# A chunked state-space scan: the running sums of the decay reach all partitions through memory instead of through TensorE

## The reference, cut to what matters

```python
a_cs = jnp.cumsum(da, axis=-1)
seg = a_cs[..., :, None] - a_cs[..., None, :]
lmat = jnp.exp(jnp.where(causal, seg, -jnp.inf))
y_diag = jnp.einsum("bgrcls,bcsgrp->bclgrp", cb[:, :, None] * lmat, x_dt)
```

## Time and profile before

| | us |
|---|---|
| median of 3 runs | 1354.4 |
| lowest, highest | 1351.99, 1354.83 |
| profiled execution, its own time | 1355.93 |
| its span in the trace | 1354.1 |
| TensorE busy | 1225.2 (90%) |
| VectorE busy | 448.6 (33%) |
| ScalarE busy | 270.8 (20%) |
| GpSimd busy | 195.4 (14%) |

### The profile page before, as it was taken

How to read it: one execution, slowest core, us unless ns; L and a number is a source line. 1 busy time by engine, 2 the same in 40 slices (tenths; PEclk the granted TensorE clock), 3 DMA queues, 4 the chain that set the end, 5 groups by cost and what they waited for, 6 DMA issues and landing times.

```text
span 1354.1 us, 13742 instructions
## 1 busy us (share of the span) xinstructions
PE 1225.2 (90%) x4939; PEld 640.7 (47%) x4939; DVE 448.6 (33%) x985; ACT 270.8 (20%) x656; POOL 195.4 (14%) x316
## 2 busy tenths in 40 slices
PE   3999999888999998999998999999998899978856
PEld 1535865556554445448843444443443344433322
DVE  4576024345556301102773222221212121211116
ACT  2141121122442000000121222221212121211101
POOL 4000011110002000001262122111121212111101
PEclk9999999888999998999998999998998999998978
DMA  9632220112437431218053989999999999999564
GB/s 303 167 125 62 74 82 32 43 52 94 125 113 268 144 129 31 93 62 348 35 202 108 362 315 395 424 422 421 420 419 396 410 405 407 377 417 419 239 254 202
DMA packets 106827, 318.08 MB, mean 235 GB/s; under 512 B 14260, under 2 KB 67592, under 8 KB 80776
## 3 DMA queue, kind: packets, MB, share of 16 engines
q1 hardware_dynamic: 87152, 269.37, 51.6%
q0 software_dynamic: 18080, 43.07, 8.9%
q10 hardware_dynamic: 1528, 4.77, 0.9%
HBM read 310.29 MB, written 26.79 MB: 249 GB/s over the span
## 4 chain that ended last, share of the span: by engine, by line
PE 81%; DVE 6%; DMA 6%; issue 3%; SPq 2%; ACT 1%; POOL 0%; POOLq 0%; ACTq 0%; DVEq 0%
PE ps L1725 21%; PE ps L1573 12%; PE ps L1733 10%; PE ps L1353 7%; PE ps L1361 5%; DMA gu_lo<-in_exp_w_up_dram 4%; PE ps L1601 4%; PE ps L1388 3%; PE ps L1713 3%; PE ps L1546 2%; PE ps L1802 2%; PE ps L1654 2%; PE ps L1510 1%; PE ps L1674 1%; PE ps L1446 1%
## 5 line engine op out<-in xcount | busy, mean ns | idle before, releaser
L1725 PE MATMUL ps<-gu_hi,xsT 128*64 128x512 f32 (+1 forms) x672 | 219.5, 614 | 24.4 <-DMA gu_hi<-in_exp_w_up_dram 11.5
L1725 PEld LDWEIGHTS ps<-gu_hi,xsT 128*64 128x64 f32 (+1 forms) x672 | 85.8, 165 | 136.9 <-issue 136.5
L1272 DVE SCALAR_TENSOR_TENSOR hid<-ps,wgt,gated 128x256 f32<-128x256 f32 x42 | 20.3, 484 | 338.8 <-ACT gated L860 338.8
L1573 PE MATMUL ps<-n1T,ring 128*128 128x512 f32 x256 | 113.0, 603 | 3.7 <-DVE mod L1098 3.0
L1725 PE MATMUL ps<-gu_lo,xsT 128*64 128x512 f32 (+1 forms) x352 | 95.5, 660 | 22.4 <-issue 16.6
L1353 PE MATMUL ps<-n1T,ring 128*128 128x512 f32 x256 | 111.9, 594 | 0.0
L1733 PE MATMUL ps<-dn_hi,hidT 128*64 128x512 f32 (+1 forms) x336 | 108.6, 596 | 0.0
L632 POOL DMA_INDIRECT expert_rows<-hn,meta x42 | 41.7, 994 | 420.7 <-DVE hn L1268 399.7
L860 ACT ACTIVATE gated<-ps 128x256 f32<-128x256 f32 x42 | 16.1, 384 | 331.9 <-PE ps L1725 331.9
L1573 PEld LDWEIGHTS ps<-n1T,ring 128*128 128x128 f32 x256 | 49.4, 194 | 65.6 <-issue 61.7
L1353 PEld LDWEIGHTS ps<-n1T,ring 128*128 128x128 f32 x256 | 48.1, 190 | 58.7 <-issue 58.7
(11 more groups left out here) (325 smaller groups left out, 1383.5 us busy)
## 6 DMA issues: line engine op xcount, KB each, us to landing
gu_hi<-in_exp_w_gate_dram SPq DMA_DIRECT2D x42, 1024.0 KB, 16.7
gu_hi<-in_exp_w_up_dram SPq DMA_DIRECT2D x42, 1024.0 KB, 28.7
dn_hi<-in_exp_w_down_dram SPq DMA_DIRECT2D x42, 1024.0 KB, 23.6
ring<-in_w_in_dram SPq DMA_DIRECT2D x24, 1024.0 KB, 5.6
gu_lo<-in_exp_w_gate_dram SPq DMA_DIRECT2D x22, 1024.0 KB, 14.0
gu_lo<-in_exp_w_up_dram SPq DMA_DIRECT2D x22, 1024.0 KB, 27.1
dn_lo<-in_exp_w_down_dram SPq DMA_DIRECT2D x22, 1024.0 KB, 21.9
h<-in_ada_w_dram POOLq DMA_DIRECT2D x32, 512.0 KB, 4.9
```

The costliest lines, as they stand in the source:

```text
L1573: ins = pe.matmul(ps[:, 4 * jj + b, :], w[:, k, P * jj:P * jj + P], src[:, k, :], start=(k == 0), stop=(k == KC - 1))
L1725: ins = pe.matmul(ps[rows, 2 + b, :], xsT[:, b, k, rows], gu(s)[:, :, k, :], start=(k == 0), stop=(k == KC - 1))
```

## The change

The running sums are also computed by four matmuls after the third z block, one per tile, with `dts` as the stationary side and the triangle as the moving side: 16 rows (one per head) of 128 columns, in bank 7 of PSUM. ScalarE copies them to `summed` (16 partitions, in the room of `attT`). GpSimd stores them to a tensor in memory, `decay_sums`, and loads them back tile by tile with a broadcast over the 128 partitions, 8 KB each, into `decay`, which lies in a part of `raw` that is free after the convolution. The load for tile t + 1 is issued when the subtractions of tile t are done. `sum_rows` is gone, and the subtractions read `decay` in SBUF.

The order in a tile on TensorE becomes: `turn_tile`, `FILL[3t]`, `outputs`, `FILL[3t+1]`, the first four of the eight matmuls of `FILL[3t+2]`, `turn_u`, and the other four. ScalarE's reads of the fills move to fit. The final sums over the experts' rows use the semaphores `x_in` in place of their own `sums_in`, with other counts. The core of the diff:

```diff
+    decay_d = nc.dram_tensor("decay_sums", [T, HEADS, P], F32, kind="Internal").ap()
...
+        decay = flat(raw[:, :, :])[:, PAIRS * SEQ:(PAIRS + T) * SEQ].rearrange("p (h l) -> p h l", h=HEADS)
+        summed = attT[0:HEADS, 0, :]
...
@@ the GpSimd queue, ahead of its loop over tiles and in it @@
+            def spread(t):
+
+                if t >= 1:
+                    pool.wait_ge(seg_done, 2 * t)
+                pool.dma_start(decay.rearrange("p h l -> p (h l)"),
+                               decay_d[t:t + 1].rearrange("t h l -> t (h l)").broadcast_to([P, HEADS * P])).then_inc(decay_in, 16)
+
+            pool.wait_ge(summed_done, 1)
+            pool.dma_start(decay_d.rearrange("t h l -> h t l"), summed.rearrange("h (t l) -> h t l", t=T)).then_inc(summed_out, 16)
+            pool.wait_ge(summed_out, 16)
+            pool.wait_ge(conv_done, NXBC)
+            spread(0)
...
                     pool.tensor_tensor(heads(xdec), heads(xdt), over(ex[:, HEADS:2 * HEADS], HD),
                                        ALU.mult).then_inc(xdec_done, 1)
+                    spread(t + 1)
@@ the ScalarE queue @@
+                    if i == 3 and t == 0:
+                        act.wait_ge(summed_ready, 1)
+                        act.activation(summed, ps[0:HEADS, 7, :], ACT.Copy).then_inc(summed_done, 1)
...
                 act.activation(ex, exarg, ACT.Exp).then_inc(ex_done, 1)
-                for n in FILL[3 * t]:
-                    evacuate(n)
                 for g in range(GROUPS):
...
-                for n in FILL[3 * t + 1]:
+                for n in FILL[3 * t]:
                     evacuate(n)
...
-                for n in FILL[3 * t + 2]:
+                for n in FILL[3 * t + 1] + FILL[3 * t + 2]:
                     evacuate(n)
@@ the VectorE queue @@
+                dve.wait_ge(decay_in, 16 * (t + 1))
+                if t >= 1:
+                    dve.wait_ge(y_ready, t)
                 for g in range(GROUPS):
-                    dve.wait_ge(bc_ready, 2 * t + g + 1)
                     for hh in range(HG):
                         hd = HG * g + hh
-                        ins = dve.tensor_scalar(seg[:, hd, :], ps[:, (6, 2)[g] + hh // 4, P * (hh % 4):P * (hh % 4) + P],
+                        ins = dve.tensor_scalar(seg[:, hd, :], decay[:, hd, :],
                                                 exarg[:, hd:hd + 1], 0.0, ALU.subtract, ALU.min)
                     ins.then_inc(seg_done, 1)
@@ the TensorE queue @@
+                if i == 2:
+                    pe.wait_ge(dtok_done, 1)
+                    for t in range(T):
+                        ins = pe.matmul(ps[0:HEADS, 7, P * t:P * t + P], dts[:, t, 1, :], tri[:, :], start=True, stop=True)
+                    ins.then_inc(summed_ready, 1)
...
-            def sum_rows(t):
-
-                for g in range(GROUPS):
-                    if g == 1:
-                        pe.wait_ge(xtok_done, t + 1)
-                    for hh in range(HG):
-                        ins = pe.matmul(ps[:, (6, 2)[g] + hh // 4, P * (hh % 4):P * (hh % 4) + P],
-                                        dts[:, t, 1, HG * g + hh:HG * g + hh + 1].broadcast_to([P, P]), tri[:, :],
-                                        start=True, stop=True)
-                    ins.then_inc(bc_ready, 1)
...
                 for n in FILL[3 * t]:
                     fill(n)
-                sum_rows(t)
+                outputs(t)
                 for n in FILL[3 * t + 1]:
                     fill(n)
-                outputs(t)
-                for n in FILL[3 * t + 2]:
+                *front, last = FILL[3 * t + 2]
+                for n in front:
                     fill(n)
+                fill(last, range(KC // 2))
                 turn_u(t)
+                fill(last, range(KC // 2, KC))
```

More of the change, by code:

```diff
@@ L318, in hybrid_ssd_swa_moe_adaln_block @@
         xdt_done, xdec_done, skip_done = sem("xdt_done"), sem("xdec_done"), sem("skip_done")
-        bc_ready, seg_done, decay_done, m_done = sem("bc_ready"), sem("seg_done"), sem("decay_done"), sem("m_done")
+        summed_ready, summed_done, summed_out = sem("summed_ready"), sem("summed_done"), sem("summed_out")
+        decay_in, seg_done, decay_done, m_done = sem("decay_in"), sem("seg_done"), sem("decay_done"), sem("m_done")
         y_ready, y_read, state_done = sem("y_ready"), sem("y_read"), sem("state_done")
@@ L350, in hybrid_ssd_swa_moe_adaln_block @@
         ht_ready, hT_done, ey_ready, ey_act, ey_dve = sem("ht_ready"), sem("hidT_done"), sem("ey_ready"), sem("ey_act"), sem("ey_dve")
-        sums_in = [sem(f"sums_in{t}") for t in range(T)]
         tail_sum, fsq_in, fin_done, stored = sem("tail_sum"), sem("fsq_in"), sem("fin_done"), sem("stored")
@@ L473, in _ @@
             for t in range(T):
-                sp.dma_start(gu(t)[:, :, :, :].rearrange("p a k f -> p (a k f)"), rows_v[:, t, 0:4 * D]).then_inc(sums_in[t], 16)
-                sp.dma_start(flat(dn(t)[:, :, :]), rows_v[:, t, 4 * D:]).then_inc(sums_in[t], 16)
+                sp.dma_start(gu(t)[:, :, :, :].rearrange("p a k f -> p (a k f)"), rows_v[:, t, 0:4 * D]).then_inc(x_in[t], 16)
+                sp.dma_start(flat(dn(t)[:, :, :]), rows_v[:, t, 4 * D:]).then_inc(x_in[t], 16)
             for t in range(T):
@@ L1320, in _ @@
                 total = dn(t)[:, 0, :]
-                dve.wait_ge(sums_in[t], 32)
+                dve.wait_ge(x_in[t], (64 if t == 0 else 48))
                 chain(dve.tensor_tensor(total, total, dn(t)[:, 1, :], ALU.add))
@@ L1347, in bank_read, with features, tokens @@
                 return proj_read[n % 2], (n - JOB_Z - (n - JOB_Z) % 2) // 2 + 1
-            def features(n, w, lo):
+            def features(n, w, lo, ks=range(KC)):
                 bank = bank_for(n)
-                for k in range(KC):
+                for k in ks:
                     ins = pe.matmul(bank, w[:, k, lo:lo + P], n1T[:, k, :], start=(k == 0), stop=(k == KC - 1))
-                ins.then_inc(proj_ready, 1)
-                return ins
-            def tokens(n, w, t):
+                if k == KC - 1:
+                    ins.then_inc(proj_ready, 1)
+            def tokens(n, w, t, ks=range(KC)):
                 bank = bank_for(n)
-                for k in range(KC):
+                for k in ks:
                     ins = pe.matmul(bank[:, 0:WB], n1T[:, k, P * t:P * t + P], w[:, k, :],
                                     start=(k == 0), stop=(k == KC - 1))
-                ins.then_inc(proj_ready, 1)
+                if k == KC - 1:
+                    ins.then_inc(proj_ready, 1)
             pe.wait_ge(const, 3)
@@ L1409, in _, with fill @@
                     ins.then_inc(dtok_ready, 1)
-            def fill(n):
+            def fill(n, ks=range(KC)):
                 if n < JOB_K:
                     m = n - JOB_Q
-                    features(n, block_in(BLK_Q + m // 2), P * (m % 2))
+                    features(n, block_in(BLK_Q + m // 2), P * (m % 2), ks)
                 elif n < JOB_V:
-                    features(n, block_in(BLK_K), P * (n - JOB_K))
+                    features(n, block_in(BLK_K), P * (n - JOB_K), ks)
                 else:
-                    tokens(n, block_in(BLK_V), n - JOB_V)
+                    tokens(n, block_in(BLK_V), n - JOB_V, ks)
             def turn_tile(t):
@@ L1797, in _ @@
             for t in range(T):
-                pe.wait_ge(sums_in[t], 32)
+                pe.wait_ge(x_in[t], (64 if t == 0 else 48))
                 rows = gu(t)[:, :, :, :].rearrange("p a k f -> p (a k f)")
```

## The result

| | us |
|---|---|
| before, median of 4 runs | 1353.45 (1351.99 to 1354.83) |
| changed, median of 4 runs | 1334.09 (1332.28 to 1335.10) |
| ratio, with its 95% interval | 0.9844 [0.9827, 0.9860] |
| changed: profiled execution, its span | 1332.7 |

The change takes 19.4 us off the median, and 21.4 us off the span of the profiled executions. The forecast was 1339.8 in a range of 1322 to 1347.

A forecast was written before the change was run, and what follows sets the result against it. TensorE, 81% of the last-ending chain, bounds the kernel; 29.7 - 1.4 - 8.7 - 5 = 14.6 us gain takes the profiled 1355.9 to 1341.3, median put at 1339.8, range 1322 to 1347.

The forecast's parts named there:

- TensorE's own work: In the scan: 14.3 us of broadcasts removed, 0.9 us for four matmuls added, net gain 13.4 us.
- waits ahead of the turned rows: TensorE's idle time before the turned rows of u in tiles 1 to 3 shrinks, gaining 6.4 us.
- waits for the next turned tile, attention's first: Half fill behind the turned rows covers 1.3 us three times, 3.9 us; wait before the attention shrinks by 0.4 us.
- clock behind the old waits: In the scan, slow TensorE work behind the removed idle times returns to faster clock, gaining 5.6 us.
- new waits ahead of the outputs: TensorE waits for the subtractions and products: 1.4 us undisturbed plus 8.7 us from GpSimd delaying VectorE, in tiles 1 to 3.
- clock behind the new waits: Slow clock after the waits before the outputs costs 2 us in tiles 1 and 2, 1 in tile 3: 5 us.
- rival 2: VectorE's subtractions are not held by GpSimd: 28.3 us gain, 1326.1 us, or 1329 at slower subtractions; chance 0.29.
- rival 1: GpSimd's delays of VectorE are real, but the new waits leave the clock up: 19.6 us gain, 1334.8 us; chance 0.16.
- the undisturbed wait: TensorE's wait before the outputs without GpSimd's delays: 0.25 us in tiles 1 and 2, 0.9 in tile 3, together 1.4.
- the attention's slow start: Clock of 0.54 at the attention's start, 331 us, expected to stay because tile 3 keeps a wait of 3.3 us.
- Rival 3: The broadcast load from memory is far slower than a block, making the kernel slower: 1363.8 us at 30 us each; chance 0.04.
- The one-to-one count past the scan: Time saved in the scan reaches the kernel's end in full, since later stages and their transfers move with it.

The follow-up runs named there:

- experiment 1: The changed kernel with GpSimd's two products of a tile held back until the tile's 16 subtractions are done; 1328.93 us, ratio 0.9807.
- experiment 9: The changed kernel with only GpSimd's skip product held back until the subtractions are done; 1335.31 us, ratio 0.9840.
- experiment 7: The changed kernel with each later broadcast load issued later, behind the root of its tile; 1332.37 us, ratio 0.9848.
- experiment 3: The changed kernel with each tile's last fill whole ahead of the turned rows of u, none behind them; 1336.28 us, ratio 0.9858.
- experiment 2: The changed kernel with the 16 broadcast matmuls per tile put back on TensorE ahead of the outputs, unread; 1336.78 us, ratio 0.9873.
- experiment 5: The kernel before, sums still broadcast by TensorE, with fills cut to the waits and ScalarE's reads reordered to fit; 1335.29 us, ratio 0.9857.

## Why the prediction was right, step by step

| step | forecast, us | measured, us |
|---|---|---|
| TensorE's own work | 13.4 | 14.3 - 1.0 = 13.3 |
| waits ahead of the turned rows | 6.4 | 2.4 + 2.4 + 1.7 = 6.5 |
| waits for the next turned tile, attention's first | 3.9 + 0.4 | 3.9 + 0.5 |
| clock behind the old waits | 5.6 | 5.6, and 0.8 + 2.3 more |
| new waits ahead of the outputs | -1.4 - 8.7 = -10.1 | -3.08 - 3.08 - 1.91 = -8.1 |
| clock behind the new waits | -5 | -2.8 - 0.2 - 0.2 = -3.2 |
| sum | 14.6 | 21.6 |

The measured terms add up to 21.6 us; the scan, the attention and the new matmuls of the span table give 21.9 + 2.0 - 1.0 = 22.9. The 1.3 us between them are not assigned. The terms come from the two profiled executions, 21.4 us apart with the 1.7 us at 33 us in it; the medians are 19.4 us apart.

The forecast's gain of 14.6 us was too small by 7.0 of these 21.6 us, all on one side: 2.0 in the new waits, 1.8 in the clock behind them, 3.1 in the clock given back. The time fell inside the range because the range reached down to rival 2; it also held rival 1, so the time by itself chose none of the three. The waits and rates in the traces did.

- The mechanism of the new wait held. GpSimd's products hold the subtraction, once each, for as long as they run (experiments 1 and 9). The forecast of about 7 us for the 16 was near the 6.53 measured; the products with C times B followed in 2.43 us as before, and TensorE started on the first half. The prediction expected gaps between the subtractions; there are none, the held ones are long. These rows agree with the rule of the Trainium skill (SBUF — State Buffer, Who interferes with whom): 1.93 and 1.94 us for an instruction of 0.27.
- The size of the waits was off by 2.0 us, mostly in the part without GpSimd. Its hold-ups are 6.53 - 3.22 = 3.3 us in tiles 1 and 2 and 4.87 - 3.22 = 1.65 in tile 3, together 8.3 for the forecast 8.7. That is already the whole 8.1 of waiting: the undisturbed wait, forecast as 1.4, was near nothing. In experiment 1 TensorE does not wait at all for the first half in tiles 1 and 2.
- One sum of the prediction is wrong. "With the rule the sum is 21.0 us" leaves out the 1.4 us of undisturbed wait; it is 29.7 - 1.4 - 8.7 = 19.6, the figure that rival 1 uses. The forecast is not touched by it.
- The larger size that was off is the clock, on both sides. I let the attention's slow start stay, because tile 3 keeps a wait of some 3.3 us; the wait stayed (3.17) and the slow start went (2.90 us for 5.20). And of three new waits only one was followed by the slow clock, with 3.68 + 3.15 us for work that takes 2.08 + 1.98. Two waits of 3.08 us in one execution had 0.50 and 1.00 behind them, experiment 7 has them the other way round, and in experiment 3 both were followed by slow work. So a rate per wait read from two or three cases was no firm price. Rival 1, in which the clock stays up, had 1334.8, and the median lies there. That is in part chance: its claim holds for two waits of three, and its 19.6 us leave out the 3.1 us of clock that came back besides and the 2.0 us less of waiting.
- The transfers cost nothing, as taken: experiment 7 moved the later three by 14 to 15 us without an effect. The bound of a 32 KB store and a 1 MB broadcast (3 and 6 us) was close to the measured 2.1 and 4.9 to 7.1. Rival 3, the slow broadcast, is out.
- Rival 2 (VectorE isn't held) is out by the two long subtractions.
- The one-to-one count past the scan held to 0.5 us.

Left open: what decides whether the clock falls behind a wait of 3.1 us, and what makes the ten matmuls at 33 us take 4.56 us or 6.2. Both vary from run to run with the same instructions.

## What to carry to other kernels

Before work is taken off the engine that sets the time, list what it was hiding: here 14.3 us of matmuls covered a chain on three other engines, and in the changed order they could be put back for about 3 us (experiment 2). Then cut the independent work to the waits in units of a matmul: that alone gave as much as the change, and both together 2.5%. And a subtraction that moved from PSUM to SBUF got faster in itself (16 of them 3.22 us for 4.23), but was then held by GpSimd's products, which it was not from PSUM in 0.6 us of overlap (experiment 5); look at what GpSimd runs beside it.

## What was unexpected of the hardware

- Held instructions show in the profile as long ones, not as idle time: 1.93 us for 0.27 us, and 4.06 for 2.43 where two-input products on VectorE stand beside GpSimd's.
- Two idle times of the same length (3.08 us) behind the same work were followed by a granted clock of 0.50 once and of 1.00 once; the 0.50 lasted less than 7 us, and cost 2.8.
- The same subtractions beside a GpSimd product are held when they read SBUF (1.94 us for 0.27) and were not in 0.6 us of overlap when they read PSUM (0.35 us at most, experiment 5).
